# Stick-breaking head pairs taken two at a time, index products on banks of their own, gate units spread out

## The reference, cut to what matters

```python
proj = u @ w_in                       # q, k, v of 8 stick-breaking heads; latent attention; indexer; gates ga, gb
# stick-breaking attention, per head and block of queries
z = q @ k.T * scale
log_keep = where(strict, log_sigmoid(-z), 0)
later = reverse_cumsum(log_keep) - log_keep
a = where(strict, exp(log_sigmoid(z) + later), 0);  y_a = a @ v
# indexer: which 64 keys a query may see in the latent ("DSA") attention
score = sum_h wi[h] * relu(qi[h] @ ki.T);  sel = top_k(score, 64)
p = softmax(q_full @ kv_all[sel].T * scale);  o_lat = p @ kv_all[sel][..., ROPE_DIM:]
y_b = o_lat @ w_uv
z = sigmoid(ga) * (y_a @ w_up_a) + sigmoid(gb) * (y_b @ w_up_b);  h = h + z @ w_o
# then a mixture of 32 experts, a retention layer with its FFN, a latent-attention layer with its FFN
```

## Time and profile before

| | |
|---|---|
| median of 3 runs | 1524.03 us (1523.28 to 1525.51) |
| the profiled execution, its own time | 1525.58 us |
| its span | 1523.8 us |
| mean granted clock of TensorE | 0.95 |
| TensorE busy | 1377.7 us, 90% of the span |
| VectorE / ScalarE / GpSimd busy | 718.7 / 527.6 / 210.7 us |
| DMA | 360.05 MB, mean 236 GB/s |

### The profile page before, as it was taken

The page is one execution under the profiler, slowest core; times in us unless marked ns, Lnnn a source line. Parts: engine busy times, 40 slices in busy tenths (PEclk is TensorE's granted clock), DMA queues, the critical chain, the costliest instruction groups (busy, mean ns, idle before and its releaser), DMA issues.

```text
span 1523.8 us, 27648 instructions
## 1 busy us (share of the span) xinstructions
PE 1377.7 (90%) x11864; PEld 1161.5 (76%) x11864; DVE 718.7 (47%) x1213; ACT 527.6 (35%) x822; POOL 210.7 (14%) x180
## 2 busy tenths in 40 slices
PE   7999899997677677766999999999999999999997
PEld 7998569754434434433987989999999986999997
DVE  5365665421112112111964675655556664565644
ACT  6346463110000001001534454444345433544342
POOL 5132003200000000000200023211224200111132
PEclk9999899799888988888999999999999999999999
DMA  9341217989999999999735242454355431354340
GB/s 364 136 161 42 98 54 305 389 375 429 427 430 429 428 428 429 429 428 424 295 125 222 111 180 83 164 197 149 122 212 188 146 125 57 151 196 191 135 170 28
DMA packets 32856, 360.05 MB, mean 236 GB/s; under 512 B 5376, under 2 KB 8448, under 8 KB 10752
## 3 DMA queue, kind: packets, MB, share of 16 engines
q1 hardware_dynamic: 32768, 358.76, 58.8%
HBM read 357.70 MB, written 1.05 MB: 235 GB/s over the span
## 4 chain that ended last, share of the span: by engine, by line
PE 72%; DMA 18%; ACT 4%; DVE 3%; issue 2%; SPq 1%; POOL 0%; DVEq 0%; ACTq 0%; POOLq 0%
PE PS L550 44%; DMA expert_w<-in_w 17%; PE PS L563 5%; PE PS L1016 4%; PE PS L1037 2%; DMA raw_x<-in_ret_qk 2%; PE PS L606 1%; DVE wl L1979 1%; PE PS L980 1%; ACT wh L1451 1%; PE PS L1192 1%; PE PS L1107 1%; PE PS L1205 1%; SPq L400 1%; PE PS L854 1%
## 5 line engine op out<-in xcount | busy, mean ns | idle before, releaser
L1979 DVE TENSOR_TENSOR wl<-raw,wh 128x4096 fp32r<-128x4096 f32 (+2 forms) x64 | 258.7, 4042 | 202.8 <-ACT wh L1451 202.7
L550 PE MATMUL PS<-UH,wh 128*128 128x272 f32 (+1 forms) x840 | 244.2, 291 | 11.7 <-DVE wl L2035 10.9
L1451 ACT ACTIVATE wh<-raw 128x4096 fp32r<-128x4096 f32 (+2 forms) x64 | 212.3, 3317 | 114.0 <-PE PS L550 108.5
L550 PE MATMUL PS<-UH,wl 128*128 128x272 f32 (+1 forms) x840 | 241.1, 287 | 0.0
L550 PE MATMUL PS<-UL,wh 128*128 128x272 f32 (+1 forms) x840 | 240.6, 286 | 0.0
L1016 PE MATMUL PS<-expert_w,XW 128*32 128x256 f32 x2048 | 155.3, 458 | 94.3 <-DMA expert_w<-in_w 94.0
L1016 PEld LDWEIGHTS PS<-expert_w,XW 128*32 128x32 f32 x2048 | 70.3, 127 | 168.4 <-DMA expert_w<-in_w 114.6
L550 PEld LDWEIGHTS PS<-UH,wh 128*128 128x128 f32 x840 | 158.8, 189 | 12.7 <-DVE wl L2035 10.9
L550 PEld LDWEIGHTS PS<-UL,wh 128*128 128x128 f32 x840 | 159.1, 189 | 0.4
L550 PEld LDWEIGHTS PS<-UH,wl 128*128 128x128 f32 x840 | 158.9, 189 | 0.0
L2346 DVE TENSOR_TENSOR SG<-PS,SG 128x128 f32<-128x128 f32 x32 | 9.3, 292 | 270.0 <-ACT SG L1720 270.0
(11 more groups left out here) (521 smaller groups left out, 3038.9 us busy)
## 6 DMA issues: line engine op xcount, KB each, us to landing
expert_w<-in_w SPq DMA_DIRECT2D x96, 2048.0 KB, 20.4
raw<-in_up SPq DMA_DIRECT2D x22, 2048.0 KB, 8.1
raw<-in_down SPq DMA_DIRECT2D x16, 1408.0 KB, 5.9
raw<-in_ret_v SPq DMA_DIRECT2D x4, 2048.0 KB, 8.3
raw<-in_ret_gate SPq DMA_DIRECT2D x4, 2048.0 KB, 8.2
raw<-in_ret_o SPq DMA_DIRECT2D x4, 2048.0 KB, 9.2
raw<-in_ret_qk SPq DMA_DIRECT2D x3, 2048.0 KB, 12.4
raw<-in_w_in_ga SPq DMA_DIRECT2D x2, 2048.0 KB, 8.4
```

The source lines that it names most:

```text
L550: mm = pe.matmul(gbank(g)[:, c0:T], w[:, c:c + P], x(k)[:, c0:], start=(k == 0 and j == 0), stop=(k == nk - 1 and j == 2))
L1451: act.activation(WH[n % 2][:, 0:w], raw(n)[:, 0:w], ACT.Copy).then_inc(hi_done, 1)
L1979: dve.tensor_tensor(wl_of(n)[:, 0:w], raw(n)[:, 0:w], WH[n % 2][:, 0:w].bitcast(F32), ALU.subtract).then_inc(lo_done, 1)
```

## The change

Five edits, all in the stage above.

1. **Order of the pairs.** Pairs 0 and 1 have their scores, then their "later" sums, then their values next to each other, and so do pairs 2 and 3. ScalarE and VectorE follow.
2. **Banks.** All index products use gbank 0 and 1. The values of pair p go to gbank 3 or 2. The last four gate units use gbank 3, 2, 0, 1, and the latent values gbank 2, 0, 1.
3. **Index products in twos**, between the other work; the last four gate units are spread: one after the scores of pairs 0 and 1, one after ten index products, two after all pairs.
4. **Tables.** ADM, WUK and WUV lie in the raw buffer of slab 9, and are loaded as soon as its low part is made. Slab 12, which uses that buffer next, is loaded after slab 11, when the last latent values are multiplied and both masks are made.
5. **Edges.** The transposes of the index weights stand before the last unit of slab 8, and ScalarE does the second sigmoid and loads its next activation tables before that unit's read-out. Keys 2 and 3 and the last latent values come behind `dsa_scores(0)`, and VectorE's last `take_best` and second mask behind its first two maxima.

```diff
-    ADM = place("ADM", [2, T], base0 + 65536 + 6 * B)
+    ADM = place("ADM", [2, T], base0)
-    WUK = region("WUK", [4, P], 8704)
-    WUV = region("WUV", [8 * HD], 10752 + 2 * B)
+    WUK = place("WUK", [4, P], base0 + 4096)
+    WUV = place("WUV", [8 * HD], base0 + 4096 + 2048)
...
         def value_bank(j):
-            return gbank((2, 3, 0)[j])
+            return gbank((2, 0, 1)[j])
...
         def index_bank(j):
-            return sbank(2 + j % 2) if j < HEADS else gbank(2 + j % 2)
+            return gbank(j % 2)
+        def pair_bank(p):
+            return gbank(3 - p % 2)
+        def last_gate_bank(u):
+            return gbank((3, 2, 0, 1)[u])
...
-            sp.wait_ge(rot_done, 10)
-            load(BND[:], a["bound"], bnd_in)
-            sp.wait_ge(unit_done, SLAB_UNITS[9])
+            sp.wait_ge(lo_done, 10)
             load(ADM[:], a["adm"], dsa_in)
             load(WUV[:], a["w_uv"], dsa_in)
             load(WUK[:], a["w_uk"], dsa_in)
-            slab(12)
+            sp.wait_ge(rot_done, 10)
+            load(BND[:], a["bound"], bnd_in)
             sp.wait_ge(sb_yd, PAIRS)
             slab(11)
+            sp.wait_ge(kv_mm, 7)
+            sp.wait_ge(ix_neg, 2)
+            slab(12)
             sp.wait_ge(yb_mm, 4)
             slab(13)
...
+            pe.wait_ge(rot_done, 7)
+            pe.wait_ge(freed["act"], FREED[UNIT0["gb"] + 2][1])
+            index_products(0, 2)
             pe.wait_ge(ka_zero, 1)
             pe.wait_ge(sb_neg, 2)
+            pe.wait_ge(rot_free, 10)
             sb_scores(0)
-
+            pe.wait_ge(rot_done, 10)
+            index_products(2, 2)
+            pe.wait_ge(tt_done, 1)
+            sb_scores(1)
             slab_ready(9)
-            pe.wait_ge(rot_done, 10)
-            for u in range(4):
-                product(UNIT0["gb"] + 4 + u, 9, 8 * u, KB, *U, c0=META)
-                if u == 0:
-                    pe.wait_ge(tt_done, 1)
-                index_products(2 * u, 2)
-                if u == 1:
-                    sb_later(0)
-            pe.wait_ge(ix_relu, HEADS)
-            sb_scores(1)
-            pe.wait_ge(freed["act"], FREED[UNIT0["gb"] + 7][1])
+            last_gate(0)
+            index_products(4, 2)
+            sb_later(0)
+            index_products(6, 2)
+            sb_later(1)
+            index_products(8, 2)
+            last_gate(1)
+            index_products(10, 2)
+            sb_scores(2)
+            sb_scores(3)
+            pe.wait_ge(freed["act"], FREED[UNIT0["gb"] + 5][1])
             sb_values(0)
-            index_products(HEADS, 4)
-            sb_later(1)
-            sb_scores(2)
             sb_values(1)
-            index_products(HEADS + 4, 4)
             sb_later(2)
-            sb_scores(3)
+            index_products(12, 2)
+            sb_later(3)
+            index_products(14, 2)
             sb_values(2)
+            sb_values(3)
+            pe.wait_ge(ix_relu, 2 * HEADS)
+            last_gate(2)
+            last_gate(3)
             expand_keys(0)
             expand_keys(1)
-            sb_later(3)
             expand_values(0)
             expand_values(1)
-            sb_values(3)
-            expand_keys(2)
-            expand_keys(3)
-            expand_values(2)
...
             dsa_scores(0)
+            expand_keys(2)
+            expand_keys(3)
+            expand_values(2)
...
@@ ScalarE
+            index_relu(0, 2)
+            hi_part(10, 0)
             sb_log(0)
+            index_relu(2, 2)
             sb_log(1)
+            last_gate(0)
+            index_relu(4, 2)
+            sb_weights(0)
+            hi_part(10, 1)
+            sb_weights(1)
+            index_relu(6, 2)
+            sb_weights(2)
+            hi_part(10, 2)
+            sb_weights(3)
+            index_relu(8, 2)
+            hi_part(10, 3)
+            last_gate(1)
+            index_relu(10, 2)
+            sb_log(2)
+            sb_log(3)
             sb_high(0)
             sb_high(1)
             sb_weights(4)
             sb_weights(5)
+            index_relu(12, 2)
+            sb_weights(6)
+            sb_weights(7)
+            index_relu(14, 2)
             sb_high(2)
+            sb_high(3)
+            last_gate(2)
+            last_gate(3)
...
@@ VectorE
             index_scores(0, 2)
+            lo_part(10, 0)
             sb_softplus(0)
-            lo_part(10, 0)
             index_scores(2, 2)
+            sb_softplus(1)
+            index_scores(4, 2)
             lo_part(10, 1)
-            index_scores(4, 2)
+            index_scores(6, 2)
+            take_best(0)
             lo_part(10, 2)
-            index_scores(6, 2)
+            index_scores(8, 2)
             lo_part(10, 3)
+            for _ in range(2):
+                take_best(0)
+            index_scores(10, 2)
+            for _ in range(3):
+                take_best(0)
             sb_softplus(2)
+            take_best(0)
+            sb_softplus(3)
+            sb_out(0)
             sb_out(1)
+            take_best(0)
+            index_scores(12, 4)
...
```

More of the change, by code:

```diff
@@ L549, in product @@
                     for j, (w, x) in enumerate(((wh, xh), (wh, xl), (wl, xh))):
[L550 removed]
+                        mm = pe.matmul(bank[:, c0:T], w[:, c:c + P], x(k)[:, c0:],
                                        start=(k == 0 and j == 0), stop=(k == nk - 1 and j == 2))
@@ L679, in _ @@
                 for u in range(4):
+                    if 4 * (n - 6) + u == 11:
+                        pe.wait_ge(rot_free, 7)
+                        pe.wait_ge(in_scaled, 10)
+                        for j, (q0, nk) in enumerate(QRY_TILES):
+                            mm = pe.matmul(sbank(2)[:, 8 * j:8 * j + 8], WIT[0:8, q0:q0 + P], ident[0:8, 0:8],
+                                           start=(j == 0), stop=True, skip_group_check=True)
+                        mm.then_inc(tt_mm, 1)
                     product(UNIT0["ga"] + 4 * (n - 6) + u, n, 8 * u, KB, *U, c0=META)
@@ L682, in _ @@
                         rotate(4 * (n - 6) + u)
[L684 to L689, removed]
             def sb_scores(p):
@@ L728, in sb_values @@
                         h = 2 * p + s
-                        mm = pe.matmul(PS[r, p % 2, q:q + w], VA[0:m, j, HD * h:HD * h + HD],
+                        mm = pe.matmul(pair_bank(p)[r, q:q + w], VA[0:m, j, HD * h:HD * h + HD],
                                        SB_A[p % 2][0:m, s, c:c + w], start=(j == 0), stop=(j == 2),
@@ L1547, in _, with gates @@
             hi(7)
-            def gates(n):
-                for u in range(4):
+            def gates(n, us=range(4)):
+                for u in us:
                     k = 4 * (n - 6) + u
@@ L1560, in _ @@
             act.activation(IDR[:], ident[:], ACT.Copy).then_inc(sb_neg, 1)
-            for n in range(6, 9):
-                gates(n)
-                if n > 6:
-                    sigmoids(GA, 4 * (n - 7))
-                if n < 8:
-                    hi(n + 2)
+            gates(6)
+            hi(8)
+            gates(7)
+            sigmoids(GA, 0)
+            hi(9)
+            gates(8, range(3))
             act.wait_ge(tt_mm, 1)
             act.activation(WI[:], sbank(2)[:, 0:16].rearrange("p (t h) -> p t h", h=8), ACT.Copy).then_inc(tt_done, 1)
+            sigmoids(GA, 4)
+            act.wait_ge(lo_done, 9)
+            act.preload_act_table_set("natural_log_exp_and_others")
+            gates(8, range(3, 4))
             def sb_log(p):
@@ L1636, in _ @@
             expanded_keys(1, 2)
-            sb_weights(6)
-            sb_weights(7)
             expanded_values(0, 3)
             expanded_values(1, 4)
-            sb_high(3)
             expanded_keys(2, 5)
@@ L2115, in sb_out @@
                 dve.wait_ge(sb_yh, p + 1)
[L2116 removed]
+                dve.tensor_tensor(YAL[:, p, META:], pair_bank(p)[:, META:T], YAH[:, p, META:].bitcast(F32),
                                   ALU.subtract).then_inc(sb_yd, 1)
             index_scores(0, 2)
+            lo_part(10, 0)
             sb_softplus(0)
[L2121 removed]
             index_scores(2, 2)
+            sb_softplus(1)
+            index_scores(4, 2)
             lo_part(10, 1)
[L2124 removed]
+            index_scores(6, 2)
+            take_best(0)
             lo_part(10, 2)
[L2126 removed]
+            index_scores(8, 2)
             lo_part(10, 3)
[L2128 to L2133 removed]
+            for _ in range(2):
+                take_best(0)
+            index_scores(10, 2)
+            for _ in range(3):
                 take_best(0)
             sb_softplus(2)
+            take_best(0)
+            sb_softplus(3)
+            sb_out(0)
             sb_out(1)
[L2137 removed]
+            take_best(0)
+            index_scores(12, 4)
+            take_best(1)
+            take_best(1)
+            sb_out(2)
+            sb_out(3)
+            for _ in range(5):
+                take_best(1)
             dve.wait_ge(dsa_in, 48)
```

(5 more changed lines are left out.)

53 lines of the change are left out of this document (14 added, 39 removed).

## The result

The changed kernel takes 1512.82 us in the median of four runs (1512.76 to 1516.40), the kernel before 1523.85 (1523.28 to 1525.51) beside it. The ratio is 0.9934, 95% interval 0.9922 to 0.9946: 11.0 us less. The profiled execution took 1512.79 us, with a span of 1511.0 us. Timed again on another occasion the same kernel had 1515.05 us against 1524.09, ratio 0.9936 (0.9917 to 0.9956), which is 9.0 us by the medians and 9.8 by the ratio. So the gain is 9 to 11 us; 11.1 had been forecast. Before the second timing I had expected 1512 to 1514 us if the gain were 11 us in every execution, and 1515 to 1518 us if the clock's part of it were not always there; 1515.05 lies at the edge of the second.

What follows compares the result with a forecast made beforehand. TensorE's attention stage was taken as the bound, with the experts' DMA stream behind it. Stage 13.0 us earlier, less 3.3 given back, plus 1.4 from the clock: 11.1 off the 1524.03 median, 1512.9 us; range 1510.5 to 1518.5.

Steps and rivals of the forecast that it cites:

- The bound: TensorE is the chain in the 56.91 us attention stage; what it saves moves the experts' DMA stream and the end in full.
- The sum of work that stays: TensorE's work from stage start to `dsa_scores(0)` at full clock: 43.3 us; with 0.6 of waits, 13.0 us earlier.
- The wait at `sb_later(2)`: TensorE's new wait before pair 2's later sums, for log and softplus, VectorE perhaps late: 0.5 us, bounds 0 and 1.5.
- What the moved work gives back: Keys 2 and 3 and last latent values still precede the first transposition, taking 3.3 us back: 9.7 us earlier.
- The second low of the clock: Half clock behind the hole at 186:189, 1.5 us lost, taken as gone: +1.4 us, bounds 0 and 1.5.
- clock 1.00 in all stretches from 128 to 190: Sign that the forecast is right: TensorE at full clock through the stage and past the first transpositions.
- The first low of the clock: TensorE at clock 0.50 throughout 162:175, after a 1.74 us idle: 6.5 us lost, to be regained.
- A: The forecast case: TensorE nearly full and clock full, 1512.9 us, bounds 1510.5 to 1516.5; chance 0.74.
- Loads: Three tables asked for ahead of the stage and slab 12 after the last latent values: free, over 25 us of cover.
- Rival B: Clock falls once between index products 10, 11 and values(3), without gate units, losing 6.5 us: 1519.4 us; chance 0.15.
- C: Clock falls at scores(2) and stays half until the gate units; 15.4 us count twice: 1528.3 us; chance 0.04.
- Rival D: An unseen wait on VectorE or in SyncE's order holds the experts' stream where it is: 1524 within 3 us; chance 0.07.

Runs made afterwards that it cites:

- e5: Changed kernel with keys 2 and 3, last latent values ahead of `dsa_scores(0)` again, and VectorE's last take_best and second mask ahead of its first maxima: 1515.93 us.
- e10: The kernel before, unchanged, profiled in a second execution: 1525.40 us (one execution).
- e11: The kernel before, unchanged, profiled in a third execution: 1523.63 us (one execution).
- e4: Changed kernel with the three tables loaded only after the last gate unit, though from their new place: 1521.78 us, ratio 0.9991 to the kernel before.
- e3: Changed kernel with gate units 3 and 4 directly behind the second one: 1520.74 us, ratio 0.9981 to the kernel before.
- e1: Kernel before with seven matmuls of ones on ones put into each of the two 1.74 us holes: 1521.07 us, ratio 0.9987.
- e12: Second profiled execution of the kernel before with its two 1.74 us holes filled by matmuls of ones: 1526.13 us (one execution).
- e2: Changed kernel with pairs 2 and 3 one after the other again on all three engines: 1526.18 us, ratio 1.0014 to the kernel before.
- e6: Changed kernel with five matmuls of ones in the 1.10 us hole before the first transposition: 1513.60 us, ratio 0.9926 to the kernel before.

## Why the prediction was right, point by point

- **The bound.** TensorE in the stage, and the stream behind it. Right: 11.06 us at the first transposition, 10.83 at the first expert load, 11.0 at the end.
- **The sum of work that stays, 43.3 us.** Between the first index products and the first latent scores are 42.69 us with a wait of 0.35 in it. The forecast for the same piece, without the transposes (0.54) and with 0.6 of waits, is 43.4. It is 0.7 too much, in small terms: two index products of 272 columns are 0.66 and not 0.7, two gate units behind one another 5.81 (161.71 to 167.52) and not 6.0, the wait 0.35 and not 0.6. The 0.27 us wait at the transposes went too, which I had not counted. So `dsa_scores(0)` came 13.9 us sooner, not 13.0.
- **The wait at `sb_later(2)`**, 0.5 with bounds 0 and 1.5: 0.35. The reason was half wrong. VectorE was in time with its rounds of take_best and waited 0.68 us for the log; the chain of log and softplus itself is longer than its cover. VectorE's row of the softplus in the changed kernel:

```profile
151.26 1.06 DVE L2115 SCALAR_TENSOR_TENSOR SB_L<-PS,SB_L 128x864 f32<-128x864 f32 x1 [0.68 <-ACT SB_L L1605]
```

- **What the moved work gives back**, 3.3: it was 5.27 - 2.39 = 2.9, and e5 shows the two sides cancel.
- **The second low of the clock**, +1.4 as gone: this step failed. The hole stayed at 1.10 us (0.9 forecast), with a second wait of 0.33 behind it, and 178:182 has 0.61. I had taken the full stretch before it as protection, and in both profiled executions of the changed kernel it is none; half clock lasts some 3.4 us there, as long as behind the hole of the kernel before. Of the signs I had named, "clock 1.00 in all stretches from 128 to 190" failed with it. The error was made good by the stage, which gave 0.9 more, and by the 0.4 less that was given back. The number is right to 0.1 us by such luck, and by the luck of the first timing: in the second the gain is 9.0 to 9.8. By its steps it was right to about 1.5.
- **The first low of the clock**, 6.5 us of gain: right for the profiled execution and for e10, wrong as a constant. In e11 it is 1.7 us, half of 3.4. The range took this in as an uncertainty of the changed kernel, while it lay in the kernel before. (The bounds that I named for A add up to 1511.3 to 1516.3 from 1524.03, not to 1510.5 to 1516.5; nothing hangs on it.)
- **Loads.** The tables were issued at 126 and slab 12 at 174.70; no engine waited for any of them. Right, and e4 gives the price of the cover: 7.6 us.
- **Rival B and C** (the clock falls in the stretch without gate units): not in any of the traces of the changed order. e3 has 22 us without a gate unit at 1.00. Behind the shortest waits of the new order, 0.35 us at `sb_later(2)`, the clock stayed at 1.00, on changing banks; the falls came behind holes of 1.10 us and more, though not behind each of them, and none behind the 0.98 us hole of e1, e11 and e12. The rule of the Trainium skill (page "TensorE: Matmul & The Clock Gate", section "A second HAM failure mode: psum-queue depth-cycling") did not show in this stage.
- **Rival D:** not seen. e3 shows how near it was: without the last two gate units as cover, VectorE sets when the first transposition can start.

## What to carry to other kernels

When three engines pass one item in a circle, take two items at a time, so that TensorE's work for the one covers the others' work for its twin; here undoing it for two of the four pairs loses all of the gain (e2). The other parts belong to it: putting the last gate units early (e3) or the tables late (e4) opens a new wait and loses 6 to 9 us in the medians. What taking two at a time would give by itself no run shows. Keep work that depends on nothing for the end of such a stage, where the slowest engine still has to catch up, and load early what stands behind it. And look at a hole on TensorE for the clock behind it as much as for its own length, in more than one execution: one profile is one draw.

## What the runs showed of the hardware

- The same holes in the same kernel were followed by 3.4 us at half clock in one execution and by 13 in two others; a hole of 1.41 us before the transpositions was followed by none, 3, or 7 us of it (e1 and e12 are one kernel). A hole of 1.10 us there was followed by some 3 us of it in the changed kernel, twice, and in e2, and by none in e4. Behind the first 1.74 us hole of the kernel before the clock stayed at 1.00 in three of three executions. Single executions of the kernel before spread over 1520.9 to 1529.7 us.
- With matmuls whose result nobody reads in the holes the clock was 1.00 from 147 to 178 in both executions of e1, and in 178:182 in the one of e6 (0.57 without them). In e1 they gave 5.45 us at the end of the stage in one execution and 1.9 in the median; filling a hole with useful work gives the hole as well.
